# Two transformer blocks, four layers, on one core: where ten groups of matrix-engine steps stand inside the GEMMs, and which of two operands is prepared first at the start

## The chip, the cores and the metric

One of the eight cores of a Trainium2 chip runs the kernel. A core has a matrix engine (TensorE, PE in the rows, with its weight loads as PEld), a vector engine (VectorE, DVE), an activation engine (ScalarE, ACT), GpSimd (POOL) and SyncE (SP), which issues most transfers. The metric is the device time of one execution in microseconds (us).

## The reference

The sequence has 256 tokens of width 2048. Two blocks of two layers each run one after the other. The first block's layers have a convolution branch and an attention branch; the second block has a layer with a forget gate (called fox below) and one with a sliding window (swa).

```python
# first block, for each of its two layers
u = rmsnorm(h, norm_g[i]) @ w_in[i]
a_val, a_glu, a_z, q, k, v, b_z = split(u)
y = depthwise_conv(a_val * sigmoid(a_glu), conv_w, width=31) + conv_b
ya = silu(layernorm(y, cln_g, cln_b)) * silu(a_z)
yb = window_attention(q, k, v, bias, sink) * silu(b_z)      # 16 heads of 64
h = h + concat(ya, yb) @ w_out[i]
h = h + rmsnorm(p[i] @ w_pe[i], pe_g[i]) * sigmoid(h @ w_pg[i])
x = rmsnorm(h, final_g)
# second block, layer 0 (fox): 32 heads, four groups of eight
q, k, v, gate, f = split(rmsnorm(x, norm_g) @ fox_w_in)
log_f = log_sigmoid(f + b_f)                                  # its running sum enters the scores
x = x + (fox_attention(q, k, v, log_f) * silu(gate)) @ fox_w_out
# second block, layer 1 (swa): 32 query heads, 4 key heads, rotary embedding
x = x + (swa_attention(q, k, v, sinks) * silu(gate)) @ swa_w_out
out = rmsnorm(x, final_g_2)
```

## The kernel before

**Arithmetic.** Every GEMM is done in three terms of a reduced format: an operand is split into a rounded high part and the low rest (`w_hi`, `w_lo` for weights, `a_hi`, `a_lo`, `b_hi`, `b_lo` for activations), and each product is hi·hi + lo·hi + hi·lo.

**Pieces and k-steps.** Weights come in pieces of 512 KB into a ring of four slots (`stage`). ScalarE rounds a piece to `w_hi` (L1521, function `rounded`), VectorE subtracts it to `w_lo` (L900, function `split`), and TensorE uses it in two k-steps of 12 matmuls each (L491). ScalarE and VectorE work three pieces ahead of TensorE, and a transfer into a slot waits until VectorE has split what was there. A chunk is one GEMM of up to eight pieces into one accumulator.

**Slots and hooks.** Everything else is placed by hand into this stream. On TensorE a chunk has a table of slots: `work={5: [...]}` stands after the sixth k-step of the chunk, and a step in it may wait for other engines. On VectorE and ScalarE a chunk has hooks: `{1: [...]}` stands behind the second `split` or `rounded` of the chunk. Each engine runs its instructions in this order, so a step that waits holds all that is behind it.

**Attention.** Heads come in lots of eight, handled in four pairs. `scores(i)` (L587) writes the scores of a pair into two banks, for which the pair before must have been read by VectorE (`biased`, L994). Then come the row maxima, the exponentials on ScalarE (L1530) and the normalisation on VectorE (`norms`, L1025). `heads(kind, values, at)` places, from slot `at` on and every second slot, `turn(i)` (L610, transposes of the weights `u`, waiting for `norms`) and `attend(i)` (L630, the product with the values, waiting for ScalarE's copy, L1586, of the transposed weights). After the last `attend` VectorE multiplies by the gate (`gated`, L1035, which also waits for ScalarE's silu of the gate) and makes the low part of the next operand.

**The norm of the convolution.** In the first block VectorE does the 31 taps of eight channel groups (L1146) in between. Then it adds the channels into `mean` (L1130). `ln_sum(0)` on TensorE (L717) sums them over partitions, VectorE subtracts (`centre`, L1215, two halves), ScalarE squares both halves (`ln_squares`, L1530, `glu<-cacc`), VectorE adds the squares (`ln_total`, L1223 and L1225), `ln_sum(1)` (L722) sums them over partitions, VectorE makes the variance (`ln_var`, L1230), GpSimd the inverse root and a diagonal matrix (L1845, L1847), and `ln_spread` (L730) brings the root to all partitions. These three TensorE steps stand in slots of the second and third chunk of the output GEMM's attention half.

**Start.** The input x is transposed on TensorE in quarters (`turn_x`, L663), ScalarE makes its high part (`x_high`, L1530), VectorE the low part (`x_low`, L1080). The first GEMM needs the first quarter's both parts and the first weight piece's both parts.

**Forget gate.** Between two chunks of the fox layer stands a small GEMM for the forget gates: 16 k-steps of three matmuls each into the bank `OB` (L780). The norm of the layer before needs two roots; `spread_rs` (L568) spreads them from the two diagonal matrices that GpSimd made (L1857 to L1862).

## Time and profile before

| what | value |
|---|---|
| device time, three runs | 1818.62 us median (1818.3 to 1821.58) |
| the profiled execution | 1819.21 us, of it a span of 1817.4 us from the first to the last instruction |
| TensorE busy | 1780.4 us (98%) |
| VectorE busy | 1312.5 us (72%) |
| ScalarE busy | 902.5 us (50%) |
| GpSimd busy | 41.9 us (2%) |
| DMA engines | 57.0% of 16 engines' span for the weights' queue |
| mean granted TensorE clock | 0.999 |

Busy time on TensorE counts matmuls whose ends are modelled, so it says where the engine had matmuls at all, not how well it used them. The times are counted from the first instruction.

### The profile page before, as it was taken

How to read it: one execution, taken by the hardware profiler on the slowest of the kernel's cores; microseconds unless marked ns; L12 is line 12 of the kernel's file. 1: busy time of each engine (PE TensorE's matmuls, PEld its weight loads, DVE VectorE, ACT ScalarE, POOL GpSimd, SP SyncE). 2: the span in 40 equal slices, each digit the busy share in tenths (PEclk: the TensorE clock that was granted, in tenths of full speed). 3: DMA queues.
4: the chain of work that ended last, by engine and by line, in shares of the span. 5: the costliest groups of instructions: out<-in, count | busy, mean ns of one | idle time of the engine just before them, and what ended most of it. 6: DMA issues, size and time to landing. Idle time of an engine off the chain costs nothing.

```text
span 1817.4 us, 35698 instructions
## 1 busy us (share of the span) xinstructions
PE 1780.4 (98%) x14365; PEld 1683.5 (93%) x14365; DVE 1312.5 (72%) x2088; ACT 902.5 (50%) x1326; POOL 41.9 (2%) x48
## 2 busy tenths in 40 slices
PE   8999999999999999999999999999999999999997
PEld 7998999999999999999999898998989999999876
DVE  7898889886779987988777755555565656666654
ACT  5333565545543455446564353545455443565553
POOL 0000000000000000000000110100000000000000
PEclk9999999999999999999999999999999999999999
DMA  7576645565656664555565656565655665545463
GB/s 234 176 209 183 186 140 172 165 198 197 193 185 210 187 191 139 157 192 180 182 196 181 198 180 203 173 196 183 185 159 157 187 185 178 154 138 157 157 191 131
DMA packets 199826, 325.54 MB, mean 179 GB/s; under 512 B 14783, under 2 KB 66191, under 8 KB 199565
## 3 DMA queue, kind: packets, MB, share of 16 engines
q1 hardware_dynamic: 197085, 320.85, 57.0%
q10 hardware_dynamic: 2608, 2.84, 0.5%
q8 instruction: 94, 1.54, 0.4%
q14 instruction: 39, 0.32, 0.1%
HBM read 320.42 MB, written 2.69 MB: 178 GB/s over the span
## 4 chain that ended last, share of the span: by engine, by line
PE 78%; DVE 15%; ACT 3%; issue 1%; DMA 1%; POOL 0%; ACTq 0%; SPq 0%; DVEq 0%; POOLq 0%
PE g L491 60%; PE g L502 9%; DVE w_lo L900 6%; DVE cacc L1146 6%; PE att L587 2%; PE att L610 2%; PE att L630 2%; ACT w_hi L1521 2%; ACT u L1530 1%; DMA stage<-in_fox_w_in_dram 0%; DVE u L1025 0%; PE att L780 0%; ACT L1530 0%; DVE q L921 0%; DMA cacc<-in_norm_g_dram 0%
## 5 line engine op out<-in xcount | busy, mean ns | idle before, releaser
L900 DVE TENSOR_TENSOR w_lo<-stage,w_hi 128x1024 fp32r<-128x1024 f32 x577 | 708.0, 1234 | 425.1 <-ACT w_hi L1521 424.6
L1521 ACT CAST w_hi<-stage 128x1024 fp32r<-128x1024 f32 x577 | 598.5, 1049 | 639.1 <-PE g L491 438.5
L491 PE MATMUL g<-a_hi,w_hi 128*128 128x256 f32 x2496 | 708.4, 284 | 5.9 <-DVE w_lo L900 4.9
L491 PE MATMUL g<-a_hi,w_lo 128*128 128x256 f32 x2496 | 696.6, 279 | 0.0
L491 PE MATMUL g<-a_lo,w_hi 128*128 128x256 f32 x2496 | 696.5, 279 | 0.0
L491 PEld LDWEIGHTS g<-a_hi,w_hi 128*128 128x128 f32 x2496 | 472.3, 189 | 20.1 <-issue 15.8
L491 PEld LDWEIGHTS g<-a_lo,w_hi 128*128 128x128 f32 x2496 | 471.9, 189 | 0.0
L491 PEld LDWEIGHTS g<-a_hi,w_lo 128*128 128x128 f32 x2496 | 470.4, 188 | 1.5 <-issue 1.2
L491 PE MATMUL g<-b_hi,w_hi 128*128 128x256 f32 x1440 | 404.9, 281 | 2.9 <-DVE w_lo L900 1.9
L491 PE MATMUL g<-b_hi,w_lo 128*128 128x256 f32 x1440 | 401.5, 279 | 0.0
L491 PE MATMUL g<-b_lo,w_hi 128*128 128x256 f32 x1440 | 401.5, 279 | 0.0
L491 PEld LDWEIGHTS g<-b_hi,w_hi 128*128 128x128 f32 x1440 | 271.8, 189 | 7.4 <-issue 4.1
L491 PEld LDWEIGHTS g<-b_lo,w_hi 128*128 128x128 f32 x1440 | 271.3, 188 | 0.0
L491 PEld LDWEIGHTS g<-b_hi,w_lo 128*128 128x128 f32 x1440 | 271.1, 188 | 0.1
L1146 DVE SCALAR_TENSOR_TENSOR cacc<-glu,cw,cacc 128x256 f32<-128x256 f32 x480 | 202.5, 483 | 0.2
L1530 ACT ACTIVATE u<-u,nbias 128x128 f32<-128x128 f32 (+1 forms) x192 | 88.0, 460 | 5.8 <-DVE nbias L1379 5.8
L1586 ACT COPY pt<-att 128x384 f32<-128x384 f32 (+1 forms) x96 | 44.5, 516 | 63.4 <-PE att L610 63.4
L502 PE MATMUL g<-w_hi,a_hi 128*128 128x512 f32 (+1 forms) x192 | 69.7, 363 | 0.0
L502 PE MATMUL g<-w_hi,a_lo 128*128 128x512 f32 (+1 forms) x192 | 68.2, 355 | 0.0
L502 PE MATMUL g<-w_lo,a_hi 128*128 128x512 f32 (+1 forms) x192 | 68.1, 355 | 0.0
L502 PE MATMUL g<-w_hi,b_hi 128*128 128x512 f32 (+1 forms) x156 | 58.0, 372 | 0.0
L502 PE MATMUL g<-w_lo,b_hi 128*128 128x512 f32 (+1 forms) x156 | 57.7, 370 | 0.0
(231 smaller groups left out, 1385.0 us busy)
## 6 DMA issues: line engine op xcount, KB each, us to landing
stage<-in_fox_w_in_dram SPq DMA_DIRECT2D x128, 512.0 KB, 3.9
stage<-in_w_in_dram SPq DMA_DIRECT2D x112, 512.0 KB, 3.8
stage<-in_swa_w_in_dram SPq DMA_DIRECT2D x72, 512.0 KB, 3.8
stage<-in_w_in_dram SPq DMA_DIRECT2D x128, 256.0 KB, 3.1
stage<-in_w_out_dram SPq DMA_DIRECT2D x64, 512.0 KB, 4.2
stage<-in_w_pg_dram SPq DMA_DIRECT2D x64, 512.0 KB, 4.0
stage<-in_fox_w_out_dram SPq DMA_DIRECT2D x32, 512.0 KB, 4.5
stage<-in_swa_w_out_dram SPq DMA_DIRECT2D x32, 512.0 KB, 4.5
```

Of the source, the lines that this page charges most:

```text
L491: mm = pe.matmul(acc[:, j * S:(j + 1) * S], w[:, slot, c0 + j * P:c0 + (j + 1) * P], xx[:, k, :], start=st and m == 0 and j % 2 == 0, stop ...
L502: mm = pe.matmul(acc[:, at:at + width], xx[:, k, b * P:(b + 1) * P], w[:, slot, col:col + width], start=st and m == 0 and (kind == "N" or ...
L587: mm = pe.matmul((SB, TB)[j % 2][:, c:c + n], q_of(j, b), keys(j)[:, 0:n], start=b == 0, stop=True, skip_group_check=True)
L610: mm = pe.transpose((TB, SB)[j % 2][:, n * P:(n + 1) * P], uw[:, j, c + kb * P:c + (kb + 1) * P], ident[:, :])
L630: mm = pe.matmul(dst[half(j):half(j) + HD, at + first * P:at + S], values(j, kb), pt[:, j % 2, n * P:(n + NB - first) * P], start=i % 2 == ...
L900: dve.tensor_tensor(w_lo[:, slot, :], stage[:, slot, :], w_hi[:, slot, :].bitcast(F32), ALU.subtract).then_inc(*t.inc("w_split"))
L1146: dve.scalar_tensor_tensor(out=cacc[:, c, :], in0=src, scalar=cw[:, c, l, k:k + 1], in1=cacc[:, c, :], op0=ALU.mult, op1=ALU.add).then_inc ...
L1521: act.copy(w_hi[:, slot, :], stage[:, slot, :]).then_inc(*t.inc("w_rounded"))
L1530: return act.activation(out, in_, func, **kw).then_inc(*t.inc(name))
L1586: act.copy(pt[:, j % 2, 0:n], (TB, SB)[j % 2][:, 0:n]).then_inc(*t.inc("t_free"))
```

## The change

Five things are moved; none is added or taken out.

1. **Start.** VectorE's and ScalarE's first weight piece (`split`, `rounded`) goes ahead of the first quarter of x instead of behind it.
2. **Scores.** `score_slots` now takes a list of slots. Of the first block's first lot of heads, the first pair's scores go from slot 3 to slot 4; all other lots keep their slots.
3. **Heads.** Three kinds of lots begin one slot (one k-step) later: the first block's first lot (from 5 to 6, one lot in each of two layers), the fox lots (from 6 to 7, four lots) and the swa lots (from 6 to 7, four lots).
4. **Norm of the convolution**, in both layers: `ln_sum(0)` goes one slot on, the two squares stand in two hooks with a weight piece between them, and `ln_total` stands one piece sooner on VectorE.
5. **Two roots.** `spread_rs` goes from the last slot of the chunk ahead of the forget GEMM into the middle of that GEMM.

```diff
@@ TensorE @@
-            def score_slots(kind, keys, at, step, extra=None):
-                return {at + step * i: [scores(kind, i, keys, extra)] for i in range(GH // 2)}
+            def score_slots(kind, keys, slots, extra=None):
+                return {s: [scores(kind, i, keys, extra)] for i, s in enumerate(slots)}
...
-                chunk("T", A, p0, work=score_slots("full", keys1(0), 3, 3, keys_there))
-                chunk("T", A, p1, work=heads("full", values1(0), 5))
+                chunk("T", A, p0, work=score_slots("full", keys1(0), (4, 6, 9, 12), keys_there))
+                chunk("T", A, p1, work=heads("full", values1(0), 6))
...
-                          work={1: {2: [ln_sum(0)]}, 2: {2: [ln_sum(1)], 6: [ln_spread]}}.get(c))
+                          work={1: {3: [ln_sum(0)]}, 2: {2: [ln_sum(1)], 6: [ln_spread]}}.get(c))
...
-            chunk("T", A, 0, ready=True, work={11: [stats(2)], 15: [spread_rs((diag, diag2))]})
+            chunk("T", A, 0, ready=True, work={11: [stats(2)]})
...
             for k in range(KT):
+                if k == KT // 2:
+                    spread_rs((diag, diag2))()
                 for m, (w, xx) in enumerate(((w_hi, A[0]), (w_lo, A[0]), (w_hi, A[1]))):
...
-                chunk("T", A, 1, work=heads("causal", fox_values, 6, [taken]))
+                chunk("T", A, 1, work=heads("causal", fox_values, 7, [taken]))
...
-                chunk("T", A, 1, work=heads("causal", swa_values, 6))
+                chunk("T", A, 1, work=heads("causal", swa_values, 7))
...
-            work = heads("causal", swa_values, 6)
+            work = heads("causal", swa_values, 7)
@@ VectorE @@
+            split()
             x_low(0)()
-            split()
             x_low(1)()
             split()
...
-                chunk({0: [add_h(p1, 0)], 1: halves(centre), 3: [ln_total]}, HP)
+                chunk({0: [add_h(p1, 0)], 1: halves(centre), 2: [ln_total]}, HP)
@@ ScalarE @@
+            rounded()
             act.wait_ge(*t.see("gains_done"))
             x_high(0)()
-            rounded()
             x_high(1)()
             rounded()
             rounded()
...
-                chunk({1: [ln_squares(0), ln_squares(1)]}, HP)
+                chunk({1: [ln_squares(0)], 2: [ln_squares(1)]}, HP)
```

The instructions themselves, as each engine has them in its program (the changed kernel has two lines more, so its line numbers are two higher behind the forget GEMM's loop):

VectorE at the start, before: `a_lo` is the low part of x, `w_lo` that of a weight piece.

```order
L1086 COPY gains<-att 128x32
L1080 SCALAR_TENSOR_TENSOR a_lo<-g,gains,a_hi 128x256 x4
L900 TENSOR_TENSOR w_lo<-stage,w_hi 128x1024
L1080 SCALAR_TENSOR_TENSOR a_lo<-att,gains,a_hi 128x256 x4
L900 TENSOR_TENSOR w_lo<-stage,w_hi 128x1024
L1048 COPY h<-g 128x1024
```

VectorE at the start, of the change:

```order
L1088 COPY gains<-att 128x32
L902 TENSOR_TENSOR w_lo<-stage,w_hi 128x1024
L1082 SCALAR_TENSOR_TENSOR a_lo<-g,gains,a_hi 128x256 x4
L1082 SCALAR_TENSOR_TENSOR a_lo<-att,gains,a_hi 128x256 x4
L902 TENSOR_TENSOR w_lo<-stage,w_hi 128x1024
L1050 COPY h<-g 128x1024
```

The first piece's `w_lo` now stands ahead of the first quarter of x; on ScalarE the first `w_hi` stands ahead of the first `a_hi` in the same way.

ScalarE in the norm of the convolution, before: `glu<-cacc` are the squares.

```order
L1680 COPY u<-att 128x1024
L1521 CAST w_hi<-stage 128x1024 x5
L1530 ACTIVATE glu<-cacc 128x4x256 x2
L1521 CAST w_hi<-stage 128x1024 x5
L1530 ACTIVATE cacc<-cacc,cvec 128x256 x4
```

ScalarE in the norm, of the change:

```order
L1682 COPY u<-att 128x1024
L1523 CAST w_hi<-stage 128x1024 x5
L1532 ACTIVATE glu<-cacc 128x4x256
L1523 CAST w_hi<-stage 128x1024
L1532 ACTIVATE glu<-cacc 128x4x256
L1523 CAST w_hi<-stage 128x1024 x4
L1532 ACTIVATE cacc<-cacc,cvec 128x256 x4
```

One rounding of a weight piece now stands between the two squares.

VectorE in the norm, before: `cacc<-att,cacc` is `centre`, `glu<-glu` and `mean<-glu` are `ln_total`, `rs<-att` is `ln_var`.

```order
L1215 SCALAR_TENSOR_TENSOR cacc<-att,cacc 128x1024 x2
L900 TENSOR_TENSOR w_lo<-stage,w_hi 128x1024 x2
L1223 TENSOR_TENSOR glu<-glu 128x4x256
L1223 TENSOR_TENSOR glu<-glu 128x2x256
L1225 TENSOR_TENSOR mean<-glu 128x256
L900 TENSOR_TENSOR w_lo<-stage,w_hi 128x1024
L1256 TENSOR_TENSOR h<-h,g 128x1024
L1230 TENSOR_SCALAR rs<-att 128x2
```

VectorE in the norm, of the change:

```order
L1217 SCALAR_TENSOR_TENSOR cacc<-att,cacc 128x1024 x2
L902 TENSOR_TENSOR w_lo<-stage,w_hi 128x1024
L1225 TENSOR_TENSOR glu<-glu 128x4x256
L1225 TENSOR_TENSOR glu<-glu 128x2x256
L1227 TENSOR_TENSOR mean<-glu 128x256
L902 TENSOR_TENSOR w_lo<-stage,w_hi 128x1024 x2
L1258 TENSOR_TENSOR h<-h,g 128x1024
L1232 TENSOR_SCALAR rs<-att 128x2
```

One of the two weight pieces ahead of `ln_total` has gone behind it; `ln_var` has as many pieces ahead of it as before.

TensorE at the forget GEMM, before: `att<-diag,ones` is the spread of the two roots, L780 the forget GEMM.

```order
L491 MATMUL g<-a_hi,w_lo 128x256
L491 MATMUL g<-a_lo,w_hi 128x256
L568 MATMUL att<-diag,ones 128x256 x2
L780 MATMUL att<-a_hi,w_hi 32x256
L780 MATMUL att<-a_hi,w_lo 32x256
```

TensorE at the same place, of the change (L782 is the forget GEMM):

```order
L782 MATMUL att<-a_hi,w_lo 32x256
L782 MATMUL att<-a_lo,w_hi 32x256
L568 MATMUL att<-diag,ones 128x256 x2
L782 MATMUL att<-a_hi,w_hi 32x256
L782 MATMUL att<-a_hi,w_lo 32x256
```

24 matmuls of the forget GEMM now stand ahead of the spread, and 24 behind it.

## Rows read from the trace of the kernel before

**Rows 1.** The page's first line.
```profile
span 1817.4 us, 35698 instructions
```

**Rows 2.** Waits on PE: who waited for whom, total us, times, longest.
```profile
PE att L722 <- DVE mean L1225: 3.3, 2, 1.8
PE att L610 <- DVE u L1025: 3.2, 7, 0.8
PE att L717 <- DVE mean L1130: 1.9, 2, 0.9
PE att L587 <- DVE q L921: 1.3, 2, 0.7
PE att L568 <- POOL diag L1862: 0.9, 1, 0.9
```

**Rows 3.** Timeline of the start: start us, us, engine, line; [idle before <- releaser].
```profile
9.17 1.66 DVE L1080 SCALAR_TENSOR_TENSOR a_lo<-g,gains,a_hi 128x256 fp32r<-128x256 f32 x4 [2.77 <-ACT a_hi L1530]
10.74 1.22 DVE L900 TENSOR_TENSOR w_lo<-stage,w_hi 128x1024 fp32r<-128x1024 f32 x1
12.10 0.55 PE L491 MATMUL g<-a_hi,w_hi 128*128 128x256 f32 x1 [1.75 <-DVE w_lo L900]
17.36 0.31 PE L491 MATMUL g<-a_hi,w_hi 128*128 128x256 f32 x1
```

**Rows 4.** Tile stage, 1.6 to 2.2 us: the first piece's transfers.
```profile
L286 SPq DMA_DIRECT2D stage<-in_w_in_dram x2: 389/426/462, 1.3 to 1.8; - x2
DMA to landing us min/median/max: 4.6/4.8/4.9
```

**Rows 5.** The chain of work that ended last: start us, us, what.
```profile
21.17 2.74 PE g L491 x24
```

**Rows 6.** Timeline, first lot's scores, first layer.
```profile
163.90 1.13 PE L587 MATMUL att<-kk,q 64*128 64x256 f32 x8 [0.68 <-DVE q L921]
169.10 0.09 DVE L994 DVE_READ_ACCUMULATOR2_ANT mx<- 128x1 f32 x1
169.40 1.14 PE L587 MATMUL att<-kk,q 64*128 64x256 f32 x8
```

**Rows 7.** Timeline of PE, first transposes of a full and a swa lot.
```profile
194.61 1.06 PE L610 MATMUL att<-ident,u 128*128 128x128 f32 x8 [0.76 <-DVE u L1025]
1551.91 0.87 PE L610 MATMUL att<-ident,u 128*128 128x128 f32 x6 [0.32 <-DVE u L1025]
```

**Rows 8.** Timeline of the norm in the first layer, all engines.
```profile
325.11 0.70 PE L717 MATMUL att<-mean,ones 128*128 128x256 f32 x2 [0.93 <-DVE mean L1130]
330.53 1.06 ACT L1530 ACTIVATE glu<-cacc 128x1024 f32<-128x1024 f32 x1 [6.56 <-DVE cacc L1215]
331.79 1.06 ACT L1530 ACTIVATE glu<-cacc 128x1024 f32<-128x1024 f32 x1 [0.19 <-DVE cacc L1215]
333.82 2.36 DVE L900 TENSOR_TENSOR w_lo<-stage,w_hi 128x1024 fp32r<-128x1024 f32 x2 [2.07 <-ACT w_hi L1521]
336.10 1.95 DVE L1223 TENSOR_TENSOR glu<-glu 128x1024 f32<-128x1024 f32 x2
338.56 0.61 PE L722 MATMUL att<-ones,mean 128*128 128x1 f32 x4 [1.82 <-DVE mean L1225]
341.11 0.16 DVE L1230 TENSOR_SCALAR rs<-att 128x2 f32<-128x2 f32 x1
343.03 0.97 POOL L1847 TENSOR_TENSOR diag<-ident,rs 128x256 f32<-128x256 f32 x1
344.77 0.59 PE L730 MATMUL att<-diag,ones 128*128 128x256 f32 x2
```

**Rows 9.** Source line L1845, the root: duration ns min/median/max.
```profile
L1845 POOL TENSOR_TENSOR rs<-rs,minus_half x7: 688/700/1612, 46.5 to 1498.1; 128x2 f32<-128x2 f32 x7
```

**Rows 10.** Timeline of PE, the two roots.
```profile
986.74 1.13 PE L568 MATMUL att<-diag,ones 128*128 128x256 f32 x4 [0.94 <-POOL diag L1862]
```

**Rows 11.** Timeline of DVE, the gate of the first swa lot.
```profile
1571.02 1.29 DVE L1035 TENSOR_TENSOR gate<-gate,att 128x512 f32<-128x512 f32 x2 [1.31 <-ACT gate L1530]
```

More of the change, by code:

```diff
@@ L752, in _ @@
                 chunk("T", A, p1)
-                chunk("T", A, p0, work=score_slots("full", keys1(0), 3, 3, keys_there))
-                chunk("T", A, p1, work=heads("full", values1(0), 5))
-                chunk("T", A, p0, work=score_slots("full", keys1(1), 3, 3, taken))
+                chunk("T", A, p0, work=score_slots("full", keys1(0), (4, 6, 9, 12), keys_there))
+                chunk("T", A, p1, work=heads("full", values1(0), 6))
+                chunk("T", A, p0, work=score_slots("full", keys1(1), (3, 6, 9, 12), taken))
                 chunk("T", A, p1, work=heads("full", values1(1), 6))
@@ L810, in fox_attention @@
             def fox_attention():
-                chunk("N", A, 0, work=score_slots("causal", fox_keys, 5, 2, taken))
-                chunk("T", A, 1, work=heads("causal", fox_values, 6, [taken]))
+                chunk("N", A, 0, work=score_slots("causal", fox_keys, (5, 7, 9, 11), taken))
+                chunk("T", A, 1, work=heads("causal", fox_values, 7, [taken]))
             with t.loop(pe, "fox", 3):
@@ L847, in _, with swa_scores @@
             swa_values = lambda j, kb: v[:, kb, 0:HD]
-            def swa_scores(at):
-                return score_slots("causal", swa_keys, at, 2, swa_there)
+            def swa_scores():
+                return score_slots("causal", swa_keys, (8, 10, 12, 14), swa_there)
             def turn_rows(g):
@@ L869, in _ @@
             with t.loop(pe, "swa", 3):
-                chunk("T", A, 0, work={4: [turn_q]} | swa_scores(8))
-                chunk("T", A, 1, work=heads("causal", swa_values, 6))
-            chunk("T", A, 0, work={4: [turn_q]} | swa_scores(8))
-            work = heads("causal", swa_values, 6)
+                chunk("T", A, 0, work={4: [turn_q]} | swa_scores())
+                chunk("T", A, 1, work=heads("causal", swa_values, 7))
+            chunk("T", A, 0, work={4: [turn_q]} | swa_scores())
+            work = heads("causal", swa_values, 7)
             chunk("N", B, 1, ready=True, order=EARLY, pieces=6, end=False, work=work)
```

## The prediction

> **What bounds the kernel now.** I read the first line of the page for the span (1817.4 us [rows 1]), then the waits on TensorE, because that engine is busy in 98% of the span: what the change can give is only what TensorE stands idle, or runs at half clock. The list is short [rows 2]: 3.3 us before `ln_sum(1)` (L722), 3.2 before the first transposes of a lot (L610, 7 times), 1.9 before `ln_sum(0)` (L717), 1.3 before a first pair's scores (L587), 0.9 before the spread of the two roots (L568). Together 10.6 us, and every one stands at a place that the change touches. The reader is to see in the timeline what was late at each place, and then what comes late next. The unit of a slot is a k-step: 24 matmuls in 2.74 us [rows 5], so 12 in 1.37 us. A step moved one slot on is covered if its input was late by less than that.
>
> The sum is made against the profiled execution. It took 1819.21 us, 1.8 outside the span, and lies 0.6 above the median of the three runs, 1818.62.
>
> **Start.** The first GEMM starts at 12.10, when VectorE has the first piece's `w_lo` done (10.74 + 1.22 = 11.96), which stood behind `a_lo` (9.17 + 1.66 = 10.83) [rows 3]. In the new order `w_lo` comes first. Its piece, issued by 1.8, is there at about 1.8 + 4.9 = 6.7 [rows 4]; I give the rounding about 1.1 and the subtraction 1.22 us, which makes 9.0 to 9.1, just ahead of 9.17, where `a_lo` started anyhow. So TensorE can start 0.14 behind 10.83, at 10.97 instead of 12.10: 1.13 us. Nothing is behind it for long: the first piece takes 12.10 to 17.36, 5.26 us, for 24 matmuls, twice a fast piece, so the second piece's `w_lo` (about 14.3) is in time. But these are matmuls at the lower clock: the row at 17.36 is the first that runs in 0.31, and I take it that this is where the granted 1.2 GHz becomes 2.4. If the rise comes 1.13 earlier too, the whole 1.13 is won; if it stays at 17.36, the 1.13 us at the start are slow ones, worth half, 0.57. If it rises earlier still, because the gap ahead of the GEMM is shorter, each microsecond of it is worth half; with no slow matmul left in the first piece at all that would be 5.26 / 2 = 2.6 more. I take 1.1, with 0.6 and 3.7 as ends. The Trainium skill speaks to this ("TensorE: Matmul & The Clock Gate", Part 1: The HAM clock gate): the chip judges activity on a schedule of its own that does not restart with the kernel, so the moment of the rise varies from run to run. By that rule a single pair of runs may show the 0.57 or more than 1.13; one trace cannot show it.
>
> **Scores.** The first pair waited 0.68 for q [rows 6]. One slot on, the wait is gone, but the second pair keeps its slot and needs the banks that VectorE reads for the first pair; that ends at 169.10 + 0.09 = 169.19, by VectorE's own pace, and the second pair started at 169.40. So at most 0.2 us is won in this layer, and the stall moves to the second pair. The second layer has a smaller margin yet (the same rows there are 0.1 apart). I take 0.15 for both, ends 0 and 1.3 (the waits of rows 2).
>
> **Heads.** The first transposes wait 0.76 in a full lot, 0.32 in a swa lot [rows 7]; the seven waits sum to 3.2 [rows 2], all below a k-step. The view counts from a matmul's modelled end, and fast matmuls start every 0.114 us [rows 5] but are shown longer (0.31 for the one of rows 3), so each stall is up to 0.2 longer than shown, and three fox lots have waits too small for the list. I take 3.5, ends 3.2 and 4.6. What is late next: the lot's last `attend` now ends about a k-step less the stall later, 1.0 us. In a swa lot VectorE's `gated` waited for ScalarE's silu, not for it, until 1571.02 [rows 11]; the last `attend` then ends near 1570.5 and still is not what is waited for. ScalarE's last copy comes 1.0 later too and holds the rounding behind it, but that piece is wanted only in the next chunk, several us later.
>
> **Norm of the convolution.** `ln_sum(0)` waited 0.93 and is now covered, about 1.0 us with the modelled end. `ln_sum(1)` waited for a chain [rows 8]: both squares on ScalarE (330.53 and 331.79, to 332.85), only then the rounding of the next piece, then two `w_lo` on VectorE (333.82, 2.36), the total (336.10) and TensorE at 338.56. Now the rounding stands between the squares: it ends near 332.5, the second square near 333.5, one `w_lo` runs from 332.6 to 333.75, and the total starts there, 2.35 us earlier. From the total's start to TensorE it takes 338.56 − 336.10 = 2.46, so `ln_sum(1)` comes at 336.2, not 338.56. TensorE, already 1.0 earlier, would arrive at 335.6: the wait falls from 1.8 to about 0.6. The `w_lo` that went behind the total is done at 337.3, and TensorE wants it at 338.1.
>
> What is late next is `ln_spread`, now at 344.77. TensorE would reach it 2.36 earlier, at 342.4. But the root starts from `ln_var` at 341.11. Between the total and `ln_var` VectorE had one `w_lo` and an addition; now it has two `w_lo`, and one takes half of the 2.36. So the total is 2.35 earlier and `ln_var` only about 1.2. The diagonal was ready at 343.03 + 0.97 = 344.00; minus 1.2 that is 342.8. So a new wait of about 0.4 stands there, and the layer wins 344.77 − 342.8 = 1.97, say 1.95, with `ln_sum(0)` in it. Both layers: 3.9. Ends: 1.9 (only `ln_sum(0)`) and 5.2 (both waits of rows 2 gone).
>
> This new wait depends on GpSimd's root, which took 0.70 us in most cases but 1.61 at the longest [rows 9], and the norm is where it is long: VectorE is in a `w_lo` then. The Trainium skill ("SBUF — State Buffer", Who interferes with whom) says that a VectorE instruction with two inputs in SBUF holds off a GpSimd instruction that reads SBUF, and that whoever starts first goes first. As the order from `ln_var` on is unchanged the root should be as long as before and the sum stays; were it free of that, the 0.9 us would end the new wait and the norm would give 4.7, not 3.9.
>
> **Two roots.** The wait of 0.94 [rows 10] goes: GpSimd is ready at about 986.7, and TensorE comes to the spread only after 24 matmuls, 2.7 us later than before. One more change of accumulator costs about 0.1. VectorE takes the roots only behind the whole GEMM. I take 0.9, ends 0 and 1.1.
>
> **Sum.** 1.1 + 0.15 + 3.5 + 3.9 + 0.9 = 9.55 us. Does it last? What is won upstream of a stretch that VectorE sets (the convolution's taps) is kept only if VectorE's work there starts from a TensorE event; each such stretch starts with an accumulator being read or a piece being released, so it moves as a whole. Against the median: 1818.6 − 9.6 = 1809.0 us.
>
> **The rivals.**
>
> 1. *Everything closes, norm bound by the root (my forecast).* 1809.0, its own range 1806.5 to 1811.5 from the start's 0.6 and 3.7 and the norm's 4.7. Chance 0.66.
> 2. *A moved piece takes back part.* The `w_lo` behind the total has only 0.8 us of margin, the first `w_lo` of the start 0.1, and the banks of the scores none. If the norm gives only its `ln_sum(0)` part (1.0 per layer) and the start half, 9.6 − 1.9 − 0.5 = 7.2; if the lots lose half of theirs too, 5.4. Time 1811.4 to 1813.2. For it: margins taken from one execution. Against it: they are worked out from the order and are positive. Chance 0.18.
> 3. *The change does not do what it says:* VectorE, not TensorE, sets the first block, so that a stall closed in one place opens as an equal one in the next, as it does for the scores. Then only the second block's lots and the roots pay, 1.3 + 0.6 + 0.9 = 2.8: 1815.8. Against it: before `ln_sum(1)` VectorE itself waited 2.07 [rows 8]. Chance 0.12.
> 4. *Slower.* The last copy of a lot stands ahead of a rounding on ScalarE and comes 1.0 us later in all ten lots. Should that rounding, and VectorE's `w_lo` behind it, become what the next chunk waits for, every lot stands a k-step, 10 × 1.37 = 13.7, against 9.6 won: 1822.7. It decides once the copy is late by more than the three pieces that the other engines are ahead, some 5 us; it is late by 1.0. Chance 0.04.
>
> **Numbers.** 1809.0 is the likeliest. From 1806.0 to 1813.5 holds the forecast and the partial case, a little over 8 in 10. A median of three runs of this kernel tells about 0.2%, 3.6 us, from no change. Faster by more than that: 0.66 + 0.18 and a little of case 3, 0.86. Within it: 0.10. Slower: 0.04.
>
> **What would show it.** In the changed kernel's trace: the first GEMM matmul near 10.97; no wait before L610 and L717; a wait of about 0.7 before the second pair's scores, releaser VectorE's `mx`; before `ln_sum(1)` about 0.6 left and before `ln_spread` a new one of 0.4, released by GpSimd's diagonal; `ln_sum(0)` to `ln_spread` 19.66 us before, near 17.4 then; none before L568. The forecast is wrong if waits on `w_lo` grow from piece to piece, if `ln_var` is not 1.2 us earlier, if q for the rotary step is late in the swa lots, or if the clock rises much earlier than its old place.

## The result: 1800.3 us, 18.3 less than before, twice what was predicted

| kernel | device time, median (range) |
|---|---|
| before | 1818.57 us (1818.3 to 1821.58) |
| changed | 1800.27 us (1799.29 to 1804.65) |
| ratio | 0.9900, 95% interval 0.9881 to 0.9920 |

The forecast was 1809.0 us, with a range of 1806.0 to 1813.5, so the direction was right and the size was not. The profiled execution of the changed kernel took 1804.65 us, 14.6 less than that of before. Measured once more beside before in another comparison, the ratio was 0.9908 (0.9885 to 0.9931).

The page's first line and the waits on TensorE of the changed kernel (its line numbers are two higher from L780 on):

```profile
span 1802.9 us, 35699 instructions
```

```profile
PE g L491 <- DVE w_lo L902: 4.5, 6, 1.7
PE g L491 <- DVE a_lo L1082: 1.1, 2, 0.8
PE att L587 <- DVE mx L996: 0.9, 1, 0.9
PE att L678 <- DVE h L1054: 0.8, 1, 0.8
PE att L730 <- POOL diag L1849: 0.7, 2, 0.5
```

All five waits of [rows 2] at the moved steps are gone. In their place stand the two spreads of the norm (0.7 us in all, as forecast) and two small waits at the start (L678 and `a_lo`), which were not.

**The norm** went as the prediction had worked it out. The timeline, to be laid beside [rows 8]:

```profile
322.03 0.59 PE L717 MATMUL att<-mean,ones 128*128 128x256 f32 x2
326.84 1.06 ACT L1532 ACTIVATE glu<-cacc 128x1024 f32<-128x1024 f32 x1 [6.21 <-DVE cacc L1217]
328.74 1.06 ACT L1532 ACTIVATE glu<-cacc 128x1024 f32<-128x1024 f32 x1
330.01 1.95 DVE L1225 TENSOR_TENSOR glu<-glu 128x1024 f32<-128x1024 f32 x2
332.48 0.61 PE L722 MATMUL att<-ones,mean 128*128 128x1 f32 x4
336.15 0.16 DVE L1232 TENSOR_SCALAR rs<-att 128x2 f32<-128x2 f32 x1
336.39 1.61 POOL L1847 TENSOR_TENSOR rs<-rs,minus_half 128x2 f32<-128x2 f32 x1 [287.86 <-DVE rs L1232]
339.11 0.70 PE L730 MATMUL att<-diag,ones 128*128 128x256 f32 x2 [0.47 <-POOL diag L1849]
```

From `ln_sum(0)` to `ln_spread` it is 17.1 us; it was 19.7, and 17.4 was forecast. The new wait is 0.47 (forecast 0.4), and GpSimd's root takes its long 1.61 us.

**Scores and roots**, timeline of TensorE:

```profile
163.07 1.13 PE L587 MATMUL att<-kk,q 64*128 64x256 f32 x8
167.12 1.14 PE L587 MATMUL att<-kk,q 64*128 64x256 f32 x8
984.37 1.02 PE L568 MATMUL att<-diag,ones 128*128 128x256 f32 x4
```

Neither pair of scores waits by more than 0.2 us in this execution. In the changed kernel's second traced execution (changed_again, below) the second pair does, as the forecast had it:

```profile
167.35 1.14 PE L587 MATMUL att<-kk,q 64*128 64x256 f32 x8 [0.57 <-DVE mx L996]
```

The two roots no longer wait.

**Where the rest came from.** I laid the two traces over each other matmul by matmul along the GEMMs (some 13,100 matmuls, the same in both) and split the distance between them into two parts: gaps between matmuls, and the spacing of matmuls that follow each other without a gap. Up to 1,070 of them stand in such a row, and within one row the spacing is constant. It has two values, 113.3 ns and 117.8 ns. The chain of waits shows both, behind the last fox lot. Before (start us, us, what):

```profile
1353.75 0.85 PE att L610 x6
1354.60 2.83 PE g L491 x24
...
1359.03 2.73 PE g L491 x24
...
1363.37 2.83 PE g L491 x24
...
1367.80 2.73 PE g L491 x24
...
1371.34 92.77 PE g L491 x786
```

The changed kernel, at the same lot:

```profile
1346.19 0.65 PE att L610 x6
1346.85 2.75 PE g L491 x24
...
1351.21 2.83 PE g L491 x24
...
1355.64 2.73 PE g L491 x24
...
1359.98 2.83 PE g L491 x24
...
1363.61 87.93 PE g L491 x774
```

92.77 / 786 is 118.0 ns a matmul, 87.93 / 774 is 113.6. The 12 matmuls more are worth 1.4 us; the other 3.5 us are the spacing. The reader is to see the pattern too: behind each step of a lot the spacing changes over (2.83, 2.73, 2.83, 2.73 for 24 matmuls), and the last one stays for the whole stretch. Before, the lot began at 117.8 (2.83); changed, at 113.3 (2.75, with the first gap in it). The granted clock is no part of the difference between these two traces: from the end of the first piece to the last microseconds neither has a fall of it. Windows of the trace (us; busy and count of PE; PEclk; DMA share; GB/s), before and then changed:

```profile
1380.00:1450.00 70.00, 70.00 (x597) 1.00 0.58 181
```

```profile
1370.00:1440.00 70.00, 70.00 (x620) 1.00 0.57 183
```

In 70 us, 597 matmuls before and 620 now, with the clock at 1.00 (the 2.4 GHz level) in both and the DMA load alike. In the profiled pair, gaps give 14.1 of the 14.5 us between the spans, and the spacing only 0.4, because it went both ways: 5.6 us won behind the fox lots, and about 4.3 lost in the 1,017 matmuls before the forget GEMM, 117.8 ns in that one execution of the changed kernel, and 0.9 in smaller pieces. Its other three executions lie 4 to 5 us lower, as they would with that stretch at 113.3.

### The profile page after: what moved, and what is told of

It is laid out like the page before. It is cut to its first block, busy times and chain, and to the rows that moved or that the text cites. A ratio compares the mean times of both kernels' runs of the same rounds, so it can differ in the third digit from the quotient of the medians.

```text
span 1802.9 us, 35699 instructions
## 1 busy us (share of the span) xinstructions
PE 1775.9 (99%) x14365; PEld 1680.5 (93%) x14365; DVE 1312.6 (73%) x2088; ACT 899.7 (50%) x1326; POOL 44.1 (2%) x48
## 4 chain that ended last, share of the span: by engine, by line
PE 83%; DVE 13%; ACT 1%; issue 1%; DMA 1%; POOL 0%; SPq 0%; ACTq 0%; DVEq 0%
PE g L491 65%; PE g L502 10%; DVE w_lo L902 5%; DVE cacc L1148 5%; PE att L587 2%; PE att L630 2%; PE att L610 2%; ACT w_hi L1523 1%; DMA stage<-in_fox_w_in_dram 0%; DMA u<-in_x_dram 0%; DVE h L1258 0%; PE att L782 0%; PE att L839 0%; ACT cacc L1532 0%; DVE glu L1225 0%
## 5 line engine op out<-in xcount | busy, mean ns | idle before, releaser
L491 PEld LDWEIGHTS g<-a_hi,w_hi 128*128 128x128 f32 x2496 | 470.0, 188 | 19.3 <-issue 14.5
```

The source lines that it names most:

```text
L491: mm = pe.matmul(acc[:, j * S:(j + 1) * S], w[:, slot, c0 + j * P:c0 + (j + 1) * P], xx[:, k, :], start=st and m == 0 and j % 2 == 0, stop ...
```

## The experiments

Each kernel ran in five rounds beside before. Kernels of one comparison share its runs of before, whose median was 1819.97 to 1824.23 with single runs from 1814.3 to 1827.8, a wider spread than in the first comparison. The comparisons ran on three chips, each kernel beside before on the same one. So I read the ratio, and the trace for what stands behind it.

| label | median, us | before | ratio (95% interval) |
|---|---|---|---|
| heads_on | 1808.49 | 1820.82 | 0.9931 (0.9915 to 0.9947) |
| norm_on | 1815.05 | 1820.82 | 0.9961 (0.9947 to 0.9975) |
| start_on | 1818.32 | 1820.82 | 0.9989 (0.9975 to 1.0004) |
| fox_back | 1809.55 | 1820.82 | 0.9933 (0.9917 to 0.9949) |
| changed_again | 1803.22 | 1819.97 | 0.9908 (0.9885 to 0.9931) |
| fox_on | 1811.23 | 1819.97 | 0.9948 (0.9931 to 0.9965) |
| last_on | 1821.08 | 1819.97 | 1.0005 (0.9989 to 1.0021) |
| spread_later | 1810.30 | 1819.97 | 0.9945 (0.9926 to 0.9964) |
| fox_five | 1814.39 | 1819.99 | 0.9966 (0.9951 to 0.9980) |
| scores_late | 1798.36 | 1819.99 | 0.9879 (0.9861 to 0.9897) |
| spread_moved | 1810.13 | 1819.99 | 0.9939 (0.9916 to 0.9962) |
| spread_moved2 | 1812.38 | 1819.99 | 0.9959 (0.9947 to 0.9972) |
| six_early | 1849.91 | 1823.60 | 1.0143 (1.0118 to 1.0168) |
| seven_waits | 1807.70 | 1823.60 | 0.9914 (0.9894 to 0.9934) |
| scores_late_again | 1807.96 | 1823.60 | 0.9911 (0.9888 to 0.9935) |
| scores_both | 1806.69 | 1823.60 | 0.9910 (0.9889 to 0.9931) |
| norms_late | 1820.86 | 1824.23 | 0.9993 (0.9976 to 1.0011) |
| spread_halves | 1805.17 | 1824.23 | 0.9891 (0.9874 to 0.9908) |

Theory A: the change gives what stalls it closes. Theory B: the place of a step also sets the spacing behind it.

### One part at a time

**heads_on**: the diff of the change's heads alone.

> The kernel before with one part of the change: all ten lots of heads one slot on (the full lot from 5 to 6, the fox lots and the swa lots from 6 to 7). Theory A: the change gives what stalls it closes and no more; laid over each other matmul by matmul, the two traces show 5.1 us of closed stalls at these ten places (0.9 in each full lot, 1.4 in the fox lots, 1.9 in the swa lots), so 1818.6 - 5.1 = 1813.5. Theory B: moving a step also decides how closely the GEMM's matmuls behind it follow each other (113.3 or 117.8 ns from start to start in the traces), and the fox lots one slot on turn their GEMMs to the closer spacing: 5.6 us more, 1807.9.

12.3 us, not 5.1; theory B's 10.7 was nearer.

**norm_on**: the diff of the norm alone.

> The kernel before with one part of the change: the norm of the convolution in both layers (ln_sum(0) a slot on, the squares in two hooks, ln_total a piece sooner). Both theories: 4.1 us, as the overlaid traces show it and near the 3.9 of the prediction: 1814.5. If VectorE's ring of pieces takes it back in the chunks behind, only the 2.0 us of ln_sum(0) stay: 1816.6.

5.8 us in the medians, 4.6 to 9.6 by the interval. The trace shows 1.2 us closed at `ln_sum(0)` and 1.5 at `ln_sum(1)` in each layer, and 0.5 lost again before `ln_spread` and 0.5 before the next chunk's operand: 3.5 in both. In the changed kernel's own trace the same places give 4.1, as was said.

**start_on**: the diff of the start alone.

> The kernel before with one part of the change: the first weight piece rounded and split ahead of x. Theory A: the first matmul comes 1.05 us sooner and the rise of the clock goes with it and further, since the gap ahead of the GEMM is shorter; 3.3 us sooner at the end of the first piece, 1.6 of it paid back by new waits on a_lo and h: net 1.6, 1817.0, and the trace shows the clock's rise before 15 us. Theory B (the rise was chance in that one execution): the first matmul 1.05 sooner, the rise near 17 as before, net 0.6 to 1.1: 1817.5 to 1818.0.

2.5 us in the medians, with an interval that holds zero. The first matmul comes at 10.90, 1.2 sooner. The trace bears out theory A's sign: the rise of the clock lies ahead of the GEMM. But theory B's reason, chance, is what the other traces show; see below on the first piece.

**fox_back**: the changed kernel with

```diff
-                chunk("T", A, 1, work=heads("causal", fox_values, 7, [taken]))
+                chunk("T", A, 1, work=heads("causal", fox_values, 6, [taken]))
```

> The changed kernel with the four fox lots of heads back at slot 6, all else as changed. Theory A (closed stalls alone): the 1.4 us of the fox lots are lost, 1800.3 + 1.4 = 1801.7, and the spacing of the matmuls behind the lots is as in the changed kernel's own trace or changes at random. Theory B (the place of the lots sets the spacing): the GEMMs behind them, 1367 to 1450 us above all, go back to 117.8 ns, 5.6 us more: 1807.3.

It lies 11.3 us below before where the changed kernel lies 16.8 to 18.3: putting back four lots costs 5.5 to 7 us, not 1.4. Its trace has 92.77 us for 786 matmuls behind the last lot, as before.

**changed_again**: the changed kernel, unchanged.

> The changed kernel itself, once more, beside the kernel before on one chip. Theory A (closed stalls, and spacing that comes by chance at every place): it lies 14 us below before in the median and its own runs spread as widely as those of before did in the last comparison, 10 us. Theory B (the spacing behind the fox lots goes by their place): 18 to 19 us below, 1800 to 1802, and its trace shows the long stretches behind all four fox lots at 113.3 ns again, while the two long stretches behind the spread of the root in the first block (1065 and 1017 matmuls) may fall either way, 4.7 us each.

16.8 us, single runs from 1800.4 to 1809.4; all four stretches behind the fox lots at 113.3 ns, the 1,017 matmuls at 117.8 again.

**fox_on**: before with the fox lots alone at 7 (the diff above, turned round).

> The kernel before with one part of the change: the four fox lots of heads from slot 6 to 7, nothing else. Theory A: the closed stalls alone, 1.4 us: 1819 where before stands at 1820.5. Theory B: those and the spacing of the stretches behind the four lots, which in the traces with slot 6 were at 117.8 ns in most cases (all four times behind the last lot, 784 matmuls or 3.5 us, and in 7 of 12 cases behind the others, 394 matmuls or 1.8 us each): 8 to 9 us in all, 1812.

8.7 us. Theory A's 1.4 fell. The trace has 87.93 us for 774 matmuls behind the last lot.

**last_on**: before, with only the last `attend` of a fox lot moved:

```diff
+            def fox_heads(at, last):
+                work = heads("causal", fox_values, at, [taken])
+                work[last] = work.pop(at + 2 * (GH // 2))
+                return work
...
-                chunk("T", A, 1, work=heads("causal", fox_values, 6, [taken]))
+                chunk("T", A, 1, work=fox_heads(6, 15))
```

> The kernel before with only the last attend of each fox lot moved, from behind slot 14 to behind slot 15, so that it stands directly ahead of the next chunk as in the changed kernel; the lots still begin at slot 6 and their stall stays. Theory A: nothing is closed, 1820.5, no change. Theory B: if the place of the last step ahead of a long stretch decides, the four stretches run at 113.3 ns and it gives 7 us: 1813.5. A third possibility: it is not the last step's place but how the lot begins (behind a stall or not), then the last stretch stays at 117.8 ns and the time as before.

No change in time, and in its chain the last stretch is slow although the step ahead of it stands exactly as in the changed kernel:

```profile
1383.17 91.36 PE g L491 x774
```

So it is not the last step's place. The third possibility, that how the lot begins decides, is left.

### What makes a lot begin slow

Two theories were left. B1: a lot whose first step waits begins slow. B2: its slot decides.

**fox_five**: the changed kernel with the fox lots at 5. **scores_late**: the changed kernel with the fox scores at (6, 8, 10, 12) and not (5, 7, 9, 11).

> The changed kernel with the four fox lots at slot 5 instead of 7. So far the spacing at the first step of a fox or swa lot was 113.3 ns in every trace with slot 7 and mostly 117.8 with slot 6, and it changes over at each of the lot's steps. Theory B1: a lot that begins behind a wait on VectorE starts at random or slow; at slot 5 the waits are longer than at 6 (about 1.4 us more each, 6 to 7 us in all), and the stretches behind the lots are mixed or slow, 7 us: 1803 + 6.5 + 7 = 1816. Theory B2: the slot's place decides (5 and 7 are an odd number of k-steps behind the chunk's begin): only the waits cost, 1809.5, and the stretches stay at 113.3 ns.

> The changed kernel with the four fox lots' scores one slot later (6, 8, 10, 12), the heads left at 7. The first transposes come as near to their norms as they did in the kernel before, so they wait again, at slot 7. B1 (the wait decides): the stretches behind the lots turn mixed or slow, 1.4 + 7 us less the 1 us of the waits on mx that it closes: 1803 + 7.4 = 1810. B2 (the slot decides): they stay at 113.3 ns, 1803.4.

fox_five: 5.6 us below before, some 11 above the changed kernel, near B1; every first transpose waited (2.09, 1.80, 1.80, 1.76 us from the matmul ahead) and all four lots began at 117.8 and ended so. scores_late did not make the wait it was meant to make, and the lots stayed at 113.3; it says nothing on B1 against B2. At the moved step it closed part of the wait on `mx` in the first fox lot: from the matmul ahead to the second pair it is 0.51 us, against 1.29 and 1.89 in the changed kernel's two traces. It was the best time so far.

**six_early**: lots at 6, scores at (4, 6, 8, 10). **seven_waits**: lots at 7, scores at (7, 9, 11, 13).

> The changed kernel with the four fox lots at slot 6 and their scores one slot earlier (4, 6, 8, 10), so that the norms are ready sooner and the first transposes may not wait at slot 6. B1 (a wait at the lot's first step makes the slow start): no wait before L610, and the lots begin at 113.3 ns, all four stretches behind them too: some 8 us better than with the lots at 6 and the scores at 5, about 1802 to 1804, with 1 to 2 us of new waits of the scores. B2 (the slot decides): as with the lots at 6 before, mostly 117.8 ns, 1809 to 1811.

> The changed kernel with the four fox lots at 7 and their scores two slots later (7, 9, 11, 13), so that the first transposes wait for the norms at slot 7, by the traces some 1 us. B1: the lots begin at 117.8 ns and so do the four stretches: 4 us of waits and 8.5 us, 1798.4 + 12.5 = 1811. B2: they stay at 113.3 ns and only the waits cost: 1802.5.

Both missed their condition. In six_early the lots waited still, and the scores, now ahead of VectorE, became what everything waited for (waits on PE):

```profile
PE att L587 <- DVE mx L996: 26.8, 14, 2.8
PE att L610 <- DVE u L1027: 1.8, 4, 0.5
```

Three of its four lots began slow, and it is 26 us slower than before. A step too early costs all of its wait, every time. The clock has a part too: behind these waits the granted clock fell six times to 0.50 (the 1.2 GHz level) for 3.4 us each. What one fall costs can be read in start_on, where there is one, behind `ln_sum(1)`:

```profile
337.00:340.30 3.30, 3.30 (x17) 0.50 0.50 159
```

There 15 matmuls start every 213 ns and not every 118, 1.4 us; six falls would be some 9 us, an estimate from that one. heads_on has two falls, fox_on and spread_moved2 one each, in the traced execution. seven_waits had no wait before L610 and all lots at 113.3.

**norms_late**: the changed kernel, lots at 7, and on VectorE

```diff
-                chunk({0: [evac(0, v_in)], 1: [norms("fox", 0)], 2: [norms("fox", 1)]})
+                chunk({0: [evac(0, v_in)], 2: [norms("fox", 0)], 3: [norms("fox", 1)]})
```

> The changed kernel with VectorE's two halves of the normalisation of a fox lot one weight piece later, so that the first transposes wait at slot 7. B1 (a wait at the lot's first step starts it slow): waits before L610 in the four fox lots, 1 to 2 us each, and the four stretches at 117.8 ns in most cases: 1802 + 6 + 7 = 1815. B2 (the slot decides): the waits alone, 1808, and the stretches at 113.3 ns.

This made the wait at slot 7. The last matmul ahead of the last lot and its first transposes in three timelines of TensorE: before, changed, norms_late.

```profile
1353.40 0.28 PE L491 MATMUL g<-a_lo,w_hi 128*128 128x256 f32 x1
1353.75 0.85 PE L610 MATMUL att<-ident,u 128*128 128x128 f32 x6
```

```profile
1345.91 0.28 PE L491 MATMUL g<-a_lo,w_hi 128*128 128x256 f32 x1
1346.03 0.82 PE L610 MATMUL att<-ident,u 128*128 128x128 f32 x6
```

```profile
1348.89 0.28 PE L491 MATMUL g<-a_lo,w_hi 128*128 128x256 f32 x1
1350.52 0.85 PE L610 MATMUL att<-ident,u 128*128 128x128 f32 x6 [1.35 <-DVE u L1027]
```

From start to start 0.35, 0.12 and 1.63 us: 0.12 is no wait at all. A wait of 0.23, as before, carries no idle mark, since it hides behind the matmul's modelled end. In norms_late two of the four lots began slow, the last among them (91.36 us for 774 matmuls). B2, by which the slot decides, fell. By its ratio it is some 16 us slower than the changed kernel, more than the 5.9 us of waits and what these two lots show. Its profiled execution was its quickest, with both long stretches of the first block (next section) fast; how they ran in the others is not known. The clock is not the reason: the mean granted clock of its 12 executions was 0.997 to 0.999.

All 20 traces together, fox lots and the first three swa lots of each, by the distance from the last matmul to the lot's first transpose:

| lots | at slots | begun at 113.3 ns | at 117.8 ns |
|---|---|---|---|
| no wait (0.12 us) | 7, all | 93 | 0 |
| wait (0.34 to 2.09 us) | 5, 6 and 7 | 12 | 35 |

The stretch behind the lot had the spacing of its begin in all but one of the 140. The spacing ahead of the lot does not explain the table: of the 93 without a wait, 48 followed matmuls at 117.8 ns and began at 113.3 all the same. Five stretches behind fox lots have a wait of their own in the middle, where TensorE came 0.22 to 0.71 us late to a piece (start to start). Behind it the spacing was another in four of the five: from 117.8 to 113.3 in before (at 1287.34), fox_five and six_early, from 113.3 to 117.8 in fox_back. The other 75 stretches held one spacing to their end.

That is the cause, as far as these runs can tell it: without a wait at the lot's first step the lot begins at 113.3 ns, a wait, however short, makes the spacing a matter of chance, slow in three cases of four here, and the steps behind it hand it on.

### The two long stretches of the first block

Behind `spread_rs` (L568) in the output GEMM stand 1,065 and 1,017 matmuls. Chain rows of before, norm_on, changed and scores_late:

```profile
392.77 121.06 PE g L491 x1068
```

```profile
391.19 125.79 PE g L491 x1068
```

```profile
855.13 120.14 PE g L491 x1020
```

```profile
854.38 115.62 PE g L491 x1020
```

4.7 and 4.5 us between one and the other. With the spread in its slot of before, 14 of the 34 in 17 traces were slow, in kernels that differ nowhere ahead of them as well as in others. They can make up to 9.3 of the 13 us by which before varies from run to run; that they do is not shown, since before was traced once.

**spread_later, spread_moved, spread_moved2**: the changed kernel with the spread of the root, or its sums, in other slots, such as

```diff
-                          work={1: [stats()], 6: [spread_rs()]} if c == 2 else None)
+                          work={1: [stats()], 7: [spread_rs()]} if c == 2 else None)
```

> The changed kernel with the spread of the root (L568) one slot on in six places of the first block: from the seventh to the eighth and last k-step of its chunk in the output GEMM and from the seventh to the eighth in the first layer's second chunk, in the second layer's from the fourth to the fifth. Behind it stand the longest uninterrupted stretches, 1065, 1017, 369 and 333 matmuls; the last two were at 117.8 ns in all six traces. Theory A (chance, or fixed by what stands there and not by the slot): the time as the changed kernel's, 1800 to 1802, the two short stretches still at 117.8. Theory B (the slot decides): some of the stretches change their spacing for good; all fast would be 3.1 us for the short ones and up to 4.7 for each long one: 1794 to 1798; if they go to slow, 1806 to 1810.

> The changed kernel with the spread of the root at other slots: in the output GEMM from 6 to 5 in the first layer, in the second its sums from 1 to 2 with the spread still at 6; in the second chunk from 6 to 8 in the first layer and from 3 to 5 in the second. One slot later they made every one of the four stretches slow. Theory B (place decides): each of the four stretches takes one spacing in all runs; all fast 1797 to 1799, all slow 1807 to 1810, and the spread of the runs' times shrinks to some 3 us. Theory A (chance everywhere but at the fox lots): 1803 with single runs from 1800 to 1809.

> As the one before, with the spread at 4 (first layer) and the sums at 2 with the spread at 7 (second layer) in the output GEMM, at 5 and 7 in the second chunk. A spread only three slots behind its sums meets the root still under way, a new wait of up to 1 us in two places. Theory B: each of the four stretches takes one spacing for good, 1798 to 1811 by which; theory A: 1803 to 1805 with single runs over 9 us.

One slot later made both stretches slow, and the runs agreed within 2.5 us (1808.4 to 1810.9): theory B for that slot. The other two variants gave fast and slow stretches and new waits ahead of the spread (1.3 us in spread_moved, 3.7 in spread_moved2); neither beat the changed kernel, and neither made its times steady.

Why one slot is mixed and the next always slow can be read from the traces. The spread needs GpSimd's diagonal. Timelines of before, ahead of its 1,065 matmuls, and of spread_later, at the same spread:

```profile
391.40 0.61 POOL L1847 TENSOR_TENSOR diag<-ident,rs 128x256 f32<-128x256 f32 x1
392.07 0.48 PE L568 MATMUL att<-diag,ones 128*128 128x256 f32 x1
```

```profile
386.35 0.61 POOL L1849 TENSOR_TENSOR diag<-ident,rs 128x256 f32<-128x256 f32 x1
388.33 0.38 PE L568 MATMUL att<-diag,ones 128*128 128x256 f32 x1
```

In before the diagonal is done at 392.01 and the spread starts 0.06 behind it, 0.22 us behind the matmul ahead; in spread_later it is done 1.4 us early and the distance is 0.12. So the slot of before hides a wait of 0.1 us. The four spreads of the first block in each of the 20 traces, ahead of the two long stretches and of the short ones of 333 and 369 matmuls, by that distance:

| spreads | followed at 113.3 ns | at 117.8 ns |
|---|---|---|
| no wait (0.12 us) | 0 | 42 |
| wait (0.22 to 3.05 us) | 23 | 15 |

As at the lots, a wait leaves the spacing to chance and no wait fixes it; but here what it is fixed to is the slow one.

**spread_halves**: each matmul of the spread as two of 128 columns.

```diff
-                        mm = pe.matmul(MB[:, i * S:(i + 1) * S], ones[:, :], root[:, :, :].rearrange("p b s -> p (b s)"),
-                                       start=i == 0, stop=True, skip_group_check=True)
+                        for b in range(NB):
+                            mm = pe.matmul(MB[:, i * S + b * P:i * S + (b + 1) * P], ones[:, :], root[:, b, :],
+                                           start=i + b == 0, stop=True, skip_group_check=True)
```

> The changed kernel with each matmul of the spread of a root (L568, 256 columns) written as two of 128 columns, in the same slots. Theory T (the spacing changes over at each step by what the step holds, as it does within a lot): the stretches of 333 and 369 matmuls, at 117.8 ns in all traces with this slot, come out at 113.3, 3.1 us, and the two long ones (1065 and 1017), mixed so far, become steady: 1797 to 1799 with a narrow spread if both go to 113.3, 1806 to 1808 if both go to 117.8. Theory A (what the step holds does not matter): 1801 to 1803 with single runs up to 1809.

The stretches of 333 and 369 stayed at 117.8, one long one was slow and one fast: theory T fell.

**scores_late_again, scores_both** (the second adds `(4, 7, 9, 12)` for the first lot's scores).

> The changed kernel with the fox lots' scores one slot later, once more, to see whether 1798.4 and its spread of 1.8 us stand. If the two long stretches of the first block take their spacing by chance and were lucky in five runs, single runs now lie 4.7 us higher, up to 1808; the floor is 1797.8, and the median 1798 to 1800. If they don't, the spread is again 2 us.

> As the one before, and in the first block's first lot the second pair's scores from slot 6 to 7, where they waited 0.57 us for mx. Theory 1 (the wait is what it costs): 0.6 us a layer, 1.2 in all, 1797.2. Theory 2 (VectorE sets the pace in that stretch, and the wait opens again at the next step): no change, 1798.4.

The 1798.4 was luck in part: now 1808.0, with both long stretches slow in the trace where both were fast before, ratio 0.9911 and not 0.9879. The two comparisons ran on different chips; no run separates that from chance. scores_both at 0.9910 is no different from it. No version is shown to beat the changed one by a measured time.

## Why the prediction was wrong, step by step

- **The sum's premise** failed: that a moved step is worth the wait it closes, or in its words that "what the change can give is only what TensorE stands idle, or runs at half clock". "I take 3.5, ends 3.2 and 4.6" for the heads was short by 9 us: heads_on gave 12.3. The traces show 5.1 of closed gaps. fox_on shows the rest for the fox lots alone, 8.7 us for 1.4 of closed gaps; counted over the traces, the remainder fits the spacing: 784 matmuls behind the last fox lot (3.5 us, slow in all 5 traces with the lots of before), 394 behind each of the others (1.8 us each, slow in 9 of 15, so 3.2), and 0.3 behind each of three swa lots (0.8 in all, slow in 13 of 15): 12.6. The prediction took "fast matmuls start every 0.114 us [rows 5]" as a constant; rows of 2.83 us for 24 matmuls stood in the same chain beside the one of 2.74, and I read one of them.
- **The size of the closed gaps** in the lots was off too, 5.1 for 3.5: it was said that stalls are up to 0.2 longer than shown, and that small ones are missing from the list; both were larger than I took them. Most fox and swa lots had such hidden waits of 0.2 to 0.6 us.
- **Norm**: right in mechanism, place and size (3.9 forecast, 4.1 in the traces, the root and the new wait as told), but for the 0.6 us left before `ln_sum(1)`, which was not there.
- **Start**: the first matmul at 11.05 (10.97 forecast). Behind it the forecast's open end was the right one. Timelines of the first matmuls: before, the third; heads_on, which has the start of before, the first three.

```profile
12.67 0.42 PE L491 MATMUL g<-a_lo,w_hi 128*128 128x256 f32 x1
```

```profile
11.98 0.36 PE L491 MATMUL g<-a_hi,w_hi 128*128 128x256 f32 x1 [1.99 <-DVE w_lo L900]
12.17 0.28 PE L491 MATMUL g<-a_hi,w_lo 128*128 128x256 f32 x1
12.29 0.28 PE L491 MATMUL g<-a_lo,w_hi 128*128 128x256 f32 x1
```

  The first piece runs at half pace in one execution and at full pace in another of the same start. With the start of before the pace rose at once in 1 of 5 traces and at 16.0 to 18.0 us in 4; with the new one at once in 6 of 15 and at 14.6 to 15.3 in 9. So it is chance in each run. The Trainium skill ("TensorE: Matmul & The Clock Gate", Part 1: The HAM clock gate) says that the moment varies from run to run, and these traces agree. The prediction called it the granted 1.2 GHz and took the row at 17.36 for the rise, and that was right, though the column of the clock seems to deny it. A window of before, over 24 matmuls at half pace:

```profile
12.20:17.20 5.00, 5.00 (x24) 1.00 1.09 284
```

  The column's 1.00 is no reading there. The trace's first record of a granted clock starts at 17.41 us, with 1.00; ahead of it there is none. In all 13 traces whose pace rose later the first record starts within 0.15 us of the change of pace, and in the 7 that were fast at once it starts ahead of the first GEMM matmul, at 9.29 to 10.40 us (9.89 in the changed kernel's own). So one of the prediction's signs of being wrong, a clock that rises much earlier, came true in that trace, by chance. At the end of the first piece the average is 15.0 us against 16.9, so about 1.8 for the 1.1 forecast; start_on's 2.5 has too wide an interval to say more, and its trace has 1.2 less of the gain behind `ln_sum(1)` than ahead of it, because of the fall of the clock shown above.
- **Roots**: 1.2 us in the traces for 0.9. **Scores**: in the changed kernel's first trace 0.7 us a layer closed, for 0.15 forecast in all, and no stall moved to the second pair, because at that point VectorE had moved 2.1 us ahead while TensorE, on 117.8 ns there, had moved only 1.5. That is the rarer case. In the 13 traces with these slots the second pair stood without a wait in the 6 of 26 places where the row of some 156 matmuls ahead of the first pair ran at 117.8 ns, and waited some 0.6 us in the 20 where they ran at 113.3. There the forecast held: the stall moves to the second pair.
- **The rivals**: none held. "Everything closes" was right as far as it went (the second pair's scores excepted), and its range ended where the spacing begins. No case had a gain beyond closed waits, and that is the fault of the range: every bound was taken from waits.

What stays open: what in TensorE makes the two spacings, why a step without a wait is followed by the close one at the lots and by the wide one at the spread, and why norms_late is slower than its trace accounts for.

## What to carry to other kernels

A small step inside a dense GEMM that waits even 0.1 us can cost more than its wait: what follows may run 4% slower until the next interruption. Slack ahead of such a step makes what follows the same in every run, but not always fast (the fox lots fast, the spread of the root slow), so try the place and read the stretch behind it. Measure the start-to-start spacing of a long row of matmuls (its time in the chain by its count), in both traces, before taking a matmul's duration as a constant. And where single runs of one kernel differ by 0.5%, one profiled pair can hide or invent several microseconds: count the stretches at each spacing before comparing.

## What the runs showed of the hardware

**Two spacings at one clock.** The groups of lines over 400 to 500 us (busy us, mean ns of one), for before at 113.3 ns and norm_on at 117.8; the last row is the only one of its three kinds of weight loads that is longer:

```profile
L491 PE MATMUL g<-a_hi,w_lo 128*128 128x256 f32 x256 | 70.8, 276 | 0.0
```

```profile
L491 PE MATMUL g<-a_hi,w_lo 128*128 128x256 f32 x256 | 72.0, 281 | 0.0
L491 PEld LDWEIGHTS g<-a_hi,w_hi 128*128 128x128 f32 x256 | 49.2, 192 | 0.0
```

Every third weight load takes 192 ns and not 188, and each matmul 281 and not 276; these are the only differences of more than 1 ns in TensorE's groups of the two stretches. The Trainium skill ("TensorE: Matmul & The Clock Gate", Back-to-back issue gap) says that in a stream of weight loads and matmuls the spacing is set by both together, which these rows agree with; it gives one value for each width, and the traces show two.

**A clock column that reads 1.00 ahead of its first record.** In the first 5 us of the first GEMM matmuls start every 213 ns and not every 113.3, and the clock's first record comes with the change, as told above.
